# Reordering ScalarE's and VectorE's queues in the attention steps of a three-block transformer kernel

## The reference, cut to what matters

```
s = einsum('bqgrd,bgqkd->bgrqk', qb, ks) * scale + rel_tab[...]
p = masked_softmax(s, dist >= 0)               # selected, windowed, compressed
o_sel = einsum('bgrqk,bgqkd->bqgrd', p, vs)
o_a = sum(stack([o_cmp, o_sel, o_win], -1) * gates, -1)
...
p = softmax(concatenate([s, sink], -1))[..., :-1]   # sliding window with sink
o_b = einsum('bgrqk,bkgd->bqgrd', p, vb)
y = concatenate([o_a, o_b], -1) @ w_out
```

## Time and profile before

| | |
|---|---|
| median of 3 runs | 1046.81 us (1046.77 to 1047.51) |
| the profiled execution | 1047.51 us, span 1045.7 us |
| TensorE busy | 995.4 us, 95% of the span |
| VectorE busy | 794.5 us, 76% |
| ScalarE busy | 559.7 us, 54% |
| TensorE's granted clock, mean | 0.986 |
| steps of the first mixer | about 68 to 175 us of the span |

### The profile page before, as it was taken

How to read it: one execution, slowest core, us unless ns; L and a number is a source line. 1 busy time by engine, 2 the same in 40 slices (tenths; PEclk the granted TensorE clock), 3 DMA queues, 4 the chain that set the end, 5 groups by cost and what they waited for, 6 DMA issues and landing times. The chain is left out here.

```text
span 1045.7 us, 21339 instructions
## 1 busy us (share of the span) xinstructions
PE 995.4 (95%) x8118; PEld 960.8 (92%) x8118; DVE 794.5 (76%) x1319; ACT 559.7 (54%) x1126; POOL 4.6 (0%) x14
## 2 busy tenths in 40 slices
PE   6999889999999999989999999999998999999996
PEld 5998679999999999979899999998988989999995
DVE  4756896788888776877778888877766858777775
ACT  2444784644444465554464444446556466776663
POOL 0100000000000000000000000000000000000000
PEclk9998999999999999989999999999999999999998
DMA  9967677388887657721648788765612324555541
GB/s 360 342 205 220 234 258 279 144 309 297 312 304 302 242 182 254 291 80 31 232 155 315 291 319 301 287 242 201 236 67 79 127 99 181 181 185 192 185 144 40
DMA packets 62409, 227.59 MB, mean 218 GB/s; under 512 B 7010, under 2 KB 7266, under 8 KB 61956
## 3 DMA queue, kind: packets, MB, share of 16 engines
q1 hardware_dynamic: 61556, 224.02, 59.6%
q0 software_dynamic: 640, 2.10, 0.8%
q10 hardware_dynamic: 144, 0.52, 0.1%
HBM read 225.04 MB, written 1.57 MB: 217 GB/s over the span
## 5 line engine op out<-in xcount | busy, mean ns | idle before, releaser
L1973 PE MATMUL bank<-hH,wH 128*128 128x258 f32 (+1 forms) x1544 | 444.2, 288 | 11.1 <-DVE hL L1334 8.1
L1974 PE MATMUL bank<-hL,wH 128*128 128x258 f32 (+1 forms) x1544 | 438.0, 284 | 0.0
L1975 PE MATMUL bank<-hH,wL 128*128 128x258 f32 (+1 forms) x1544 | 436.4, 283 | 0.0
L1269 DVE TENSOR_TENSOR wL<-raw,wH 128x1024 fp32r<-128x1024 f32 x270 | 328.2, 1221 | 40.5 <-ACT wH L807 39.3
L1973 PEld LDWEIGHTS bank<-hH,wH 128*128 128x128 f32 x1544 | 292.4, 189 | 18.8 <-issue 10.1
L807 ACT ACTIVATE wH<-raw 128x1024 fp32r<-128x1024 f32 x270 | 276.6, 1048 | 42.7 <-PE bank L1975 24.1
L1975 PEld LDWEIGHTS bank<-hH,wL 128*128 128x128 f32 x1544 | 293.7, 190 | 0.0
L1974 PEld LDWEIGHTS bank<-hL,wH 128*128 128x128 f32 x1544 | 293.1, 190 | 0.4
L1973 PE MATMUL bank<-aH,wH 128*128 128x256 f32 x592 | 169.2, 286 | 3.0 <-DVE wL L1269 3.0
L1975 PE MATMUL bank<-aH,wL 128*128 128x256 f32 x592 | 168.8, 285 | 0.0
L1974 PE MATMUL bank<-aL,wH 128*128 128x256 f32 x592 | 168.8, 285 | 0.0
(11 more groups left out here) (337 smaller groups left out, 1148.5 us busy)
## 6 DMA issues: line engine op xcount, KB each, us to landing
raw<-in_weights SPq DMA_DIRECT2D x270, 512.0 KB, 4.5
modbuf<-in_mod_w SPq DMA_DIRECT2D x69, 512.0 KB, 6.0
modbuf<-in_w_ada SPq DMA_DIRECT2D x36, 512.0 KB, 6.3
strips<-in_mod_w SPq DMA_DIRECT2D x16, 512.0 KB, 7.1
strips<-in_w_ada SPq DMA_DIRECT2D x12, 512.0 KB, 6.4
strips<-bias_table POOLq DMA_DIRECT2D x8, 256.0 KB, 6.4
otok<-in_cmp_w SPq DMA_DIRECT2D x4, 512.0 KB, 9.0
raw<-in_mod_w SPq DMA_DIRECT2D x2, 512.0 KB, 4.5
```

Source lines behind the costliest of these rows:

```text
L1269: V.tensor_tensor(wL[:, slot, :], raw[:, slot, :], wH[:, slot, :].bitcast(F32), ALU.subtract).then_inc(lo_ready[c], 1)
L1973: mm(out, lhs_h, rhs_h, start=start, stop=False, skip_group_check=True)
L1974: mm(out, lhs_h, rhs_l, start=False, stop=False, skip_group_check=True)
L1975: return mm(out, lhs_l, rhs_h, start=False, stop=stop, skip_group_check=True)
```

## The change

Two reorderings, no work added or taken away.

In ScalarE's steps 9 to 12 `ab_take_pt(2 * s - 2)` moves from behind the split to ahead of it. On VectorE, the call of `jobs_upto` between `ab_weigh` and the low features is gone, and the one at the end of a step runs all jobs that the step is due. So in steps 1, 2, 4, 5, 7, 8, 9 and 11 the second of two jobs moves from behind `ab_weigh` of the next step to ahead of it, right behind the first. Steps 0, 3, 6, 10 and 12 to 14 keep their order. SyncE's program is unchanged, but its loads follow the jobs' ends.

```diff
                 for f in range(8):
                     if AB_FT_STEP[f] == s - 1:
                         ab_features_high(f)
-                split_upto(ab_split(s))
                 if 9 <= s <= 12:
                     ab_take_pt(2 * s - 2)
+                split_upto(ab_split(s))
                 if s < 12:
                     ab_exp(2 * s)
                     ab_exp(2 * s + 1)
...
                 if 1 <= s <= 12:
                     ab_weigh(s - 1)
-                    jobs_upto(ab_jobs(s - 1))
                 for f in range(8):
                     if AB_FT_STEP[f] == s - 1:
                         ab_features_low(f)
...
-                jobs_upto(min(ab_jobs(s), ab_jobs(s - 1) + 1) if 1 <= s <= 11 else ab_jobs(s))
+                jobs_upto(ab_jobs(s))
```

## The result

The changed kernel takes **1055.47 us** (median of 4 runs, 1054.76 to 1055.60) against 1046.97 us (4 runs, 1046.77 to 1047.51): a ratio of 1.0072, 95% interval 1.0056 to 1.0088, so 5.9 to 9.2 us slower. The forecast was 1051.8 us with a range up to 1054.4. The sign was right; the time lies 3.7 us above the forecast and 1.1 above the range. The profiled execution took 1056.86 us, with a span of 1055.1 us, 9.4 us more than that of before. In all runs of this document two executions lie far apart from the rest, 2322.88 us of the kernel before and 1608.15 us of e13_keep9, and the ratios leave them out (the medians do not).

A forecast was written before the change was run, and what follows sets the result against it. First mixer's steps 9 to 12 were taken as bound by a three-engine loop; delays of 0.4, 1.0, 0.9, 0.45, 1.6 and 0.6 gave 5.0 us on 1046.81, so 1051.8 us, range 1048.0 to 1054.4.

The forecast's parts named there:

- A loop through three engines with hardly any slack: First mixer, steps 9 to 12: TensorE, ScalarE and VectorE wait on one another; ScalarE's reordering lengthens 6.25 us to 6.7.
- rival 1: Slack in the first mixer's loop takes most of the delay: only +1.3 us, 1048.1 us; chance 0.18.
- Step 4, +0.4: First mixer: later weighing delays the exponentials and the copy that TensorE waits 3.4 us for, costing 0.4 us.
- Steps 8 to 11, 1.0 + 0.9 + 0.45 + 1.6: First mixer: added delays in us ahead of turn(16), pv(8), pv(9) and pv(10), in that order.
- Step 12, +0.6: First mixer's end: splits behind the take, then VectorE's splits and jobs, make pv(11) 0.6 us later, 5.0 in all.
- Price 0 to 0.9 ... I take 0 in the sum: Lower clock may follow the 2.5 us wait ahead of turn(22), costing 0 to 0.9 us; counted only in the range.
- rival 3: Clock falls after each longer pause: 1.5 us at step 9 and 1.5 at step 12 on top; 1054.8 us; chance 0.13.
- Step 5, "no other is late": First mixer: one job transfer waits at most 0.3 us, on slack; others land in time (median 4.3 us); cost 0.
- The forecast for part 2 alone: First mixer with only VectorE's jobs moved: +1.6 us in all, 0.4 of it in step 4.
- I found nothing later that could take it up: Stages after the first mixer: its delay reaches the kernel's end in full.
- The base: Whole kernel before: median of three runs, 1046.81 us, to which the 5.0 us were added.
- Rival 2: Steps 9 to 12 become faster, all 2.9 us of TensorE's waits could go: 1043.9 us; chance 0.05.

The follow-up runs named there:

- e13_keep9: Kernel before with the VectorE reordering except step 9's second job, plus filler matmuls ahead of turn(16) and turn(22): 1047.94 us, ratio 1.0013.
- Part 1 alone: Kernel before with only ScalarE's take moved ahead of the split in steps 9 to 12: 1051.25 us, ratio 1.0033.
- e1: The run of Part 1 alone, against the kernel before: 1051.25 us, ratio 1.0033.
- e3: Kernel before with 56 more small matmuls ahead of the norm behind the first mixer, a plain delay: 1057.72 us, ratio 1.0099.
- e9: Kernel before, unchanged, traced again: first mixer's end 0.55 us later than in its first trace, reckoned from turn(9).
- e12: Kernel before with only step 8's second job moved ahead of the weighing: ratio 1.0003.
- e7: Changed kernel with 7 filler matmuls ahead of turn(16) and 11 ahead of turn(22): 1051.45 us (12 runs), ratio 1.0036 to the kernel before.
- e6: Changed kernel itself, unaltered, timed and traced again beside the kernel before: ratio 1.0074.
- part 2 alone: Kernel before with only VectorE's jobs moved ahead of the weighing, ScalarE as before: 1052.72 us, ratio 1.0049.
- e2_dve: The run of part 2 alone, against the kernel before: 1052.72 us, ratio 1.0049.
- e11: Kernel before with the VectorE reordering, plus 7 filler matmuls ahead of turn(16) and 5 ahead of turn(22): 1050.76 us, ratio 1.0013.
- e10: Kernel before with copy L1081 ahead of step 5's exponentials, plus 7 filler matmuls ahead of turn(16): 1044.72 us, ratio 0.9977.
- e5: Changed kernel with 12 filler matmuls ahead of turn(16) and 20 ahead of turn(22): 1056.31 us, ratio 1.0079 to the kernel before.

## Why the prediction was right and wrong

1. *"A loop through three engines with hardly any slack"*: right. Part 1 alone costs what the loop said, and rival 1 (slack takes most) is out.
2. *Step 4, +0.4*: right. With VectorE's job begun at 107.94 before and 107.98 after, `turn(9)` starts at 114.13 and 114.69: 0.5 us. It is the same in every trace: from the reduction `cm<-rstd` of this step to `turn(9)` it is 7.75 or 7.76 us in the five traces with step 4's jobs as before (before, e1, e3, e9, e12), and 8.27 or 8.28 in the seven with both jobs ahead.
3. *Steps 8 to 11, 1.0 + 0.9 + 0.45 + 1.6*: right. With the clock kept up (e7) they measure 1.25 + 1.1 + 0.45 + 1.8. Each is off by less than the noise; together they are 0.7 more than forecast.
4. *Step 12, +0.6, and the clock, "Price 0 to 0.9 ... I take 0 in the sum"*: **this is the step that failed.** The queues' share is right (0.7 in e7), but step 12 took 2.2 and 2.6 us in the two traces of the changed kernel. I looked at waits that had brought the lower clock (2.5 us and more) and at waits that had not (below 1 us), and took the free end for the waits of 1.45 and 2.5 us in my own schedule. Both turned out longer (1.8 and 2.7), and both brought it, 10 us in all. The first cost almost nothing (step 9 is 1.4 and 1.3 us with it, 1.1 without, in e7); the second fell where I had named a cover of 0.6 us, and it lasted until 165 instead of for 3 us, through the output tiles of which TensorE had nothing to spare. e6 is 2.1 us longer than e7 between `turn(9)` and the mixer's end. So the pieces are 0.5 us in step 4, 5.4 by the queues from `turn(9)` on and 2.1 by the clock, 8.0 in all, where the changed kernel's median is 7.5 above before's on its chip; that is within the noise of these differences. The total is that of rival 3 (+8.0, chance 0.13), which I had held for a side case, but not its account: of its 1.5 us at step 9 the traces show 0.1 to 0.3. The medians of e6 and e7 differ by 4.0 us, though, their traces at the end only by 1.9; the other 2 us are not settled. They may be chance of the later stages' clock, which was not shown.

   My rule by the length of the wait was not enough either. The trace of before has a low stretch with no long wait ahead of it: from 68 to 77 us TensorE stands still for 0.47 us in all, and at 77.6 its clock falls while it works.

```profile
68.00:77.00 9.00, 8.53 (x169) 7.83 (x169) 4.62 (x15) 5.22 (x14) 0.00 (x0) 1.00 0.01 5
...
78.00:79.00 1.00, 1.00 (x6) 1.00 (x6) 0.97 (x8) 0.66 (x3) 0.00 (x0) 0.50 1.20 213
```

5. *Step 5, "no other is late"*: wrong, and hidden in the changed kernel. In part 2 alone the transfer of step 9's second job costs 2.0 us. In the changed kernel VectorE waits 1.70 us for the split, until 139.96, before the jobs; the transfer lands at 141.00, and the job does not wait for it. So the two parts are not additive: alone they cost 3.1 and 3.7 us with the clock kept up in part 2, together 5.4. The forecast for part 2 alone (1.2 from `turn(9)`) was near only without that transfer (1.7 in e13, with the fillers too). The one late transfer that step 5 did name, at most 0.3 us of wait left, waited 0.46 us in the changed kernel and 1.60 in e2_dve, but on slack: `turn(16)` is 1.3 and 1.4 us late with 1.60 and with 0.46 us of it (e2_dve, e13). I took the median landing time, 4.3 us, for that of a transfer which shares its time with two others. The Trainium skill (DMA: Bandwidth & Descriptors, "Issuing engines are not separate DMA queues") says that all transfers run on the same 16 engines and interleave. The trace agrees: in e2_dve from 130 to 145 us the job pieces took 5.2 us and the weight units 6.4, in the kernel before 4.2 and 5.2 (medians). For e2_dve:

```profile
modbuf<-in_mod_w SPq DMA_DIRECT2D x4, 512.0 KB, 5.2
raw<-in_weights SPq DMA_DIRECT2D x3, 512.0 KB, 6.4
```

6. *"I found nothing later that could take it up"*: right (e3: 10.3 us in at the norm, 10.4 behind the third mixer).
7. *The base.* The first runs of before were close together (1046.77 to 1047.51), and I read that as its scatter. On the other chips 17 to 29 runs gave medians of 1047.26 to 1048.36 and single values from 1044.5 to 1052.9. Against a base of about 1048 the changed kernel is 7.5 us slower and not 8.5. Its own scatter is as wide: three more executions on record, outside the median, took 1051.67, 1053.86 and 1055.16 us. So of the 3.7 us between forecast and measurement about 2.1 are the clock, 0.9 the queues' terms and 1.0 the base; they add up to 4.0, as the noise allows.

Rival 2 (faster) had nothing for it: `weigh` starts in every step right behind the jobs. In the changed kernel the split never runs in the idle time ahead of the take, where it ran before (142.40), so ScalarE's queue did keep its order.

## What to carry over

When a reordering lengthens a wait of TensorE, price the wait and the clock behind it apart: the first by the queues, the second by stretches at the lower clock in the trace, with a chance and not with zero, and ask what the engine has to do right after it. A moved job drags its transfer: take the landing time at its new place, beside the transfers issued with it, not the median of the stage. And the best order is found from the wait: the copy that TensorE waits longest for goes ahead of work that is needed later (here 2.4 per mille). This change did the opposite: part 1 put an instruction that has to wait ahead of one that was ready, part 2 put jobs ahead of the weights that TensorE waits for.

## What the runs showed of the hardware

- Waits of TensorE of 1.8, 1.9, 2.5 and 2.7 us were followed by stretches at 1.2 GHz of 3.4 to 6.8 us, and one of 1.43 us (e2_dve) too, while one of 2.44 (`turn(9)` of the changed kernel), one of 1.64 us (e11) and, ahead of `L2262`, one of 2.78 us (e7, at 84.82, clock 1.00 to 89.8) were not. In these traces waits from 1.4 to 2.8 us went either way, and the clock also fell where TensorE had waited for only 0.47 us in the nine us before (before, at 77.6).
- With equal waits the same stage of the same kernel ran 3.3 us longer in one execution than in another, by the granted clock alone (9.12 and 12.37 us above). The scatter of whole executions was 8 us among 19 runs of before; that the clock makes most of it is likely, but was not shown.
- Filling a wait of TensorE with small matmuls (0.22 us each in float32) took 4 us off one kernel (e7) and nothing off another (e10). Behind none of the filled waits of e5, e7, e10, e11 and e13 did the clock fall. It pays where TensorE has no slack right behind the wait, and fillers longer than the wait cost their surplus (e5).
